# Where `hidh` and `hidl` lie in SBUF: two allocations moved behind `work`

## The reference

```python
for layer in range(DEPTH):
    h = h + 0.5 * swiglu(rms_norm(h, ...), w_gate, w_up, w_down)      # 1024 -> 2816 -> 1024
    h = h + mixer(rms_norm(h, ...))
    h = h + 0.5 * swiglu(rms_norm(h, ...), w_gate, w_up, w_down)
def swiglu(x, w_gate, w_up, w_down):
    return (jax.nn.silu(x @ w_gate) * (x @ w_up)) @ w_down
```

## Time and profile before

| | |
|---|---|
| median of 3 runs | 1972.77 us (1972.48 to 1973.28) |
| profiled execution | 1972.77 us |
| its span, first to last instruction | 1971.0 us |
| TensorE busy | 1960.5 us, 9838 matmuls |
| VectorE busy | 1199.4 us |
| ScalarE busy | 1018.6 us |
| mean granted TensorE clock | 1.000 |

### The profile page before, as it was taken

How to read it: one execution, slowest core, us unless ns; L and a number is a source line. 1 busy time by engine, 2 the same in 40 slices (tenths; PEclk the granted TensorE clock), 3 DMA queues, 4 the chain that set the end, 5 groups by cost and what they waited for, 6 DMA issues and landing times.

```text
span 1971.0 us, 26229 instructions
## 1 busy us (share of the span) xinstructions
PE 1960.5 (99%) x9838; PEld 1652.8 (84%) x9838; DVE 1199.4 (61%) x1817; ACT 1018.6 (52%) x1590; POOL 68.9 (3%) x77
## 2 busy tenths in 40 slices
PE   9999999999999999999999999999999999999999
PEld 7888988888888898888888898888888888888887
DVE  6555656556655566555755566655576555876554
ACT  6444555445554665444544447544475444755442
POOL 0100300000000000000000000000010000200000
PEclk9999999999999999999999999999999999999999
DMA  9655436553655426555555434555446553306550
GB/s 339 210 202 174 150 108 214 192 191 130 221 184 178 144 77 212 192 192 171 188 181 186 162 138 139 203 192 192 171 163 234 183 189 128 108 24 212 192 192 22
DMA packets 241050, 338.91 MB, mean 172 GB/s; under 512 B 5728, under 2 KB 206351, under 8 KB 240831
## 3 DMA queue, kind: packets, MB, share of 16 engines
q1 hardware_dynamic: 239710, 335.84, 50.5%
q0 software_dynamic: 496, 1.23, 0.2%
q10 hardware_dynamic: 752, 0.61, 0.1%
HBM read 336.61 MB, written 1.05 MB: 171 GB/s over the span
## 4 chain that ended last, share of the span: by engine, by line
PE 95%; DVE 2%; ACT 2%; DMA 1%; issue 0%; SPq 0%; POOL 0%; ACTq 0%
PE A L535 11%; PE A L537 11%; PE A L536 11%; PE G L535 10%; PE G L537 10%; PE G L536 10%; PE X L535 8%; PE X L537 8%; PE X L536 8%; PE A L1226 1%; PE A L904 1%; PE G L964 1%; PE X L964 1%; PE X L1210 1%; PE G L1238 1%; DVE wl L496 0%
## 5 line engine op out<-in xcount | busy, mean ns | idle before, releaser
L496 DVE TENSOR_TENSOR wl<-raw,wh 128x1024 fp32r<-128x1024 f32 (+1 forms) x553 | 653.8, 1221 | 121.3 <-ACT wh L487 120.3
L487 ACT ACTIVATE wh<-raw 128x1024 fp32r<-128x1024 f32 (+1 forms) x553 | 561.9, 1058 | 144.1 <-PE A L537 102.6
L535 PE MATMUL G<-wh,xh 128*128 128x512 f32 (+1 forms) x814 | 322.1, 396 | 0.2
L537 PE MATMUL G<-wh,xl 128*128 128x512 f32 (+1 forms) x814 | 317.2, 390 | 0.0
L536 PE MATMUL G<-wl,xh 128*128 128x512 f32 (+1 forms) x814 | 316.3, 389 | 0.0
L535 PE MATMUL X<-wh,xh 128*128 128x512 f32 x672 | 265.8, 395 | 0.3 <-DVE wl L496 0.3
L537 PE MATMUL X<-wh,xl 128*128 128x512 f32 x672 | 262.3, 390 | 0.0
L536 PE MATMUL X<-wl,xh 128*128 128x512 f32 x672 | 261.6, 389 | 0.0
L537 PEld LDWEIGHTS G<-wh,xl 128*128 128x128 f32 x814 | 152.8, 188 | 32.3
L535 PEld LDWEIGHTS G<-wh,xh 128*128 128x128 f32 x814 | 152.9, 188 | 30.9 <-DVE xl L2399 0.6
L536 PEld LDWEIGHTS G<-wl,xh 128*128 128x128 f32 x814 | 153.1, 188 | 29.9
(11 more groups left out here) (487 smaller groups left out, 2787.5 us busy)
## 6 DMA issues: line engine op xcount, KB each, us to landing
raw<-in_ffn_w_in SPq DMA_DIRECT2D x88, 1024.0 KB, 6.8
raw<-in_ffn_w_down SPq DMA_DIRECT2D x44, 1024.0 KB, 6.5
raw<-in_ffn_w_out SPq DMA_DIRECT2D x44, 1024.0 KB, 7.1
raw<-in_ffn_w_gate SPq DMA_DIRECT2D x42, 1024.0 KB, 5.5
raw<-in_ffn_w_up SPq DMA_DIRECT2D x42, 1024.0 KB, 7.5
raw<-in_a_w_in SPq DMA_DIRECT2D x12, 1024.0 KB, 6.1
raw<-in_ab_w_in SPq DMA_DIRECT2D x8, 1024.0 KB, 6.8
raw<-in_kv_w SPq DMA_DIRECT2D x6, 1024.0 KB, 6.5
```

The lines of the kernel that those rows point to most:

```text
L487: nc.scalar.activation(hi, r, ACT.Copy).then_inc(hi_done[u], 1)
L496: nc.vector.tensor_tensor(lo, r, hi.bitcast(F32), ALU.subtract).then_inc(lo_done[u], 1)
L535: nc.tensor.matmul(o, sh, rh, start=start, stop=False)
L537: return nc.tensor.matmul(o, sl, rh, start=False, stop=stop)
```

## The change

Two calls of `sb` are moved from behind `ml` to behind `work`. Nothing else is changed.

```diff
         mh = sb("mh", [P, KC, S], F32R)
         ml = sb("ml", [P, KC, S], F32R)
-        hidh = sb("hidh", [P, 2, 2 * S], F32R)
-        hidl = sb("hidl", [P, 2, 2 * S], F32R)
         const = sb("const", [P, NCONST])
         const_r = sb("const_r", [P, P + 8 + 10 * P], F32R)
         gain = sb("gain", [P, NGAIN])
         pe_col = sb("pe_col", [P, CMP_BLOCK + KC])
         work = sb("work", [P, 2304])
+        hidh = sb("hidh", [P, 2, 2 * S], F32R)
+        hidl = sb("hidl", [P, 2, 2 * S], F32R)
         arena = sb("arena", [P, ARENA])
```

## The result

The changed kernel takes 1986.59 us, median of 5 runs (1985.67 to 1987.43), against 1972.71 us before (1972.41 to 1973.28). The ratio is 1.0068, with a 95% interval of 1.0057 to 1.0080: 13.9 us slower, clear of noise. The prediction said no change, 1971.2 to 1974.4 us.

A forecast was written before the change was run, and what follows sets the result against it. The prediction took TensorE to bound the kernel, busy for 1960.5 of 1971.0 us. Its four terms, all 0, added to 1972.77 us gave 1972.8 us, with a range of 1971.2 to 1974.4 us.

The forecast's parts named there:

- What the change does to the program: Whole program: only start addresses differ, by multiples of 64 bytes, so only distance or an address above 64 bytes can matter.
- part 1: Down projection, weight loads from `hidh` and `hidl`: 188 ns each with 38 ns to spare, so cost 0.
- the closing sentence of the prediction: Any access: the forecast is wrong if cost depends on address in a way the places read don't show; no size.
- part 2: Short matmuls behind a turn (four transposes) reading `work` and `const`: cost 0, bound 2.6 us either way.
- Parts 2, 3 and 4: Short matmuls reading `work` and `const`; ScalarE and VectorE writes of `hidh`, `hidl`; DMA loads of constants: each cost 0.
- The slower rival: Down projection: writes to `work`, now beside `hid`, disturb loads from `hid`; 8.2 us more, 1981.0 us; chance 5%.
- The faster rival: Behind each turn: 46 ns are contention between `hid` writes and `xh`, `xl` reads; up to 4.1 us saved, 1968.7; chance 3%.

The follow-up runs named there:

- e2: Against the kernel before, only `pe_col` (160 bytes) put in front of `hidh`, so `hid` starts 160 bytes higher and `work` stays: 1989.67 us.
- e9: Against the kernel before, `pe_col` (160 bytes) put between `wl` and `h`: `h` to `hid` start 160 bytes higher, `wh` and `wl` do not: 2007.11 us.

## Why the prediction was wrong

**The step that failed** stands under "What the change does to the program" and goes on in part 1. I reduced the change to "each tensor keeps its start within a line of 64 bytes", and concluded that only what depends on distance or on an address above 64 bytes can change. The conclusion was true and the danger was in it: 17792 is 128 modulo 256, and the closing sentence of the prediction named just this gap without a price or a chance for it. I then held that nothing does depend on it, because loads from many places showed one number. But the comparison for the down projection had no spread in the one quantity that counts. `xh`, `hidh` and the weights were all on multiples of 256 against each other, so "32 KB lower, same 188 ns" could not tell. The comparison of part 2 did have spread, `h` at 0 and `work` at 128 against `const`, but it compared the length of loads of 140 ns, and the loads of `hidh` show that this length hardly moves when the pace does.

**Part 1 also looked at the wrong number.** The cost was bounded by the duration of a load, 188 to at most 192 ns, with 38 ns to spare. The loads stayed at 188 ns in the mean; the pace went from 0.2267 to 0.2329 us. The term set at 0 measured 12.0 us in the trace; 2112 x 6.2 ns would be 13.1 us, and the last two blocks of each network lose less. The slack of 38 ns would cover a longer load. It says nothing of starts that move apart while each load keeps its length, and this is what the runs showed.

**Parts 2, 3 and 4** held: the loads of the turn at 140 ns, the writes at 382 and 419 ns, no new wait. The sum of the change is in the one term.

**The slower rival** had the sign and about the stage, but not the mechanism. It gave 8.2 us on 815 matmuls under the writes to `work`; the down projections are slow throughout, with or without writes, and e2 makes them slow with `work` where it was. It had its check in the prediction ("over 0.232 us a matmul while `work` is written") and passed it, for another reason. A reading that only looks under the writes would have called it right.

**The faster rival** fell by its own row: 1.85 us behind a turn, not 1.81.

The section of the Trainium skill that the prediction drew on ("SBUF — State Buffer", "Who interferes with whom") knows one cause of contention, the port pair that VectorE and GpSimd share. As to engines against each other the traces agree: 0.2267 us under the writes to `work`, and in e9 a pace of 0.2333 that needs no other engine. But by the same rule the place of `hid` is worth nothing, and the runs show 0.2267 against 0.2333 at one address of `hidh`. Here the measurement decides.

**What is shown and what is argued.** Shown: the pace depends on the difference of the starts of the two operands, modulo 256 bytes, and on no single address, neighbour, engine or DMA. Argued only: that the load of the next stationary operand and the stream of the moving one meet in the memory at the same moment. They do overlap in time, as these rows of the changed kernel show:

```profile
51.12 0.39 PE L535 MATMUL A<-mh,hidh 128*128 128x512 f32 x1
51.13 0.19 PEld L536 LDWEIGHTS A<-ml,hidh 128*128 128x128 f32 x1
```

But they overlap in the kernel before as well. It also fits that the starts fall into a fixed rhythm (it repeats after three starts for 160, two for 64, seven for 128), but no run took the load away to see the loss go.

## What to carry to other kernels

When TensorE sets the time and each matmul has its own weight load, the place of tensors in SBUF is a parameter of the program: keep stationary and moving operands on starts that differ by a multiple of 256 bytes (shown here for fp32r, with loads of 128 columns and streams of 512), and look at every tensor of an odd size that is put between them. If a change only moves allocations, work out the difference of starts for each pair of operands before and after, and ask of every row that shows "the place doesn't matter" whether the difference varied in it at all. And price by the distance between starts, since durations of overlapped instructions can stay the same while the stream slows down.

## What the hardware showed that I had not expected

- The pace of a 128x512 fp32r matmul with its own 128x128 load is 0.2267 us when the two starts differ by a multiple of 256 bytes, and 0.2289 to 0.2333 us at the other six differences tried, up to 2.9% more.
- The starts fall into a fixed rhythm that goes with the difference; for 128 it is the same in two kernels with `hid` at addresses 15104 bytes apart.
- No difference tried is faster than 0, so the kernel before stood on the best of the seven tried by nothing but the sizes of its tensors.
